# A hybrid attention and expert step: 160 prompt tokens in the first output and query pass, 96 with the samples

## The reference

```
mix = [stick_breaking attention (8 heads), sparse attention (8 heads)]       # prompt and samples
h   = layer_norm(ALPHA * x + mix @ w_out)                                     # "output pass"
q   = (h @ w_query) as 8 heads x 2 halves of 128;  s = q @ sub_keys           # "query pass"
top 16 of 128 for each half; 16 x 16 sums; top 16 of these 256                # "selection", 8 heads
    -> 128 experts per token, gate = softmax of their scores
act = gelu(u_tab[expert] . h);   y = sum over experts of gate * act * v_tab[expert]
out = layer_norm(ALPHA * h + y)
```

## Time and profile before

| | |
|---|---|
| median of 3 runs | 2565.51 us |
| the profiled execution | 2565.83 us |
| its span, first to last instruction | 2564.0 us |
| PE, DVE, POOL, ACT busy | 74%, 49%, 28%, 13% |
| moved by DMA | 964.23 MB, 376 GB/s over the span |
| u and v gathers | 288 + 288, 59.7% of the DMA time |
| chain that ended last | DMA 47%, PE 34%, DVE 8% |

### The profile page before, as it was taken

The page is one execution under the profiler, slowest core; times in us unless marked ns, Lnnn a source line. Parts: engine busy times, 40 slices in busy tenths (PEclk is TensorE's granted clock), DMA queues, the critical chain, the costliest instruction groups (busy, mean ns, idle before and its releaser), DMA issues.

```text
span 2564.0 us, 29141 instructions
## 1 busy us (share of the span) xinstructions
PE 1894.7 (74%) x9494; PEld 1079.4 (42%) x9494; DVE 1248.9 (49%) x2349; ACT 335.7 (13%) x787; POOL 719.3 (28%) x594
## 2 busy tenths in 40 slices
PE   8999999979999877757776663665563545988336
PEld 5777766544478654534554310221120002655000
DVE  0510122253048867677887535434433345477860
ACT  0000111422031000201100101101110010011011
POOL 0000000000002533334333324324534246434562
PEclk9999999989999989978999876777685665555556
DMA  9889979896349999999999999999999999999998
GB/s 397 301 344 358 371 274 379 340 374 257 121 184 361 395 409 409 408 411 412 409 409 410 410 397 410 410 397 392 416 385 397 421 421 422 421 421 414 417 420 342
DMA packets 213687, 964.23 MB, mean 376 GB/s; under 512 B 23937, under 2 KB 89474, under 8 KB 122818
## 3 DMA queue, kind: packets, MB, share of 16 engines
q0 software_dynamic: 84512, 627.05, 59.7%
q1 hardware_dynamic: 93074, 300.33, 30.7%
q10 hardware_dynamic: 35952, 35.01, 4.0%
HBM read 955.81 MB, written 14.88 MB: 379 GB/s over the span
## 4 chain that ended last, share of the span: by engine, by line
DMA 47%; PE 34%; DVE 8%; issue 4%; SPq 2%; ACTq 2%; POOL 1%; ACT 1%; POOLq 0%; DVEq 0%
DMA sb<-in_peer_u,sb 20%; DMA sb<-in_peer_v,sb 19%; PE bank L1038 14%; PE bank L1344 4%; DMA sb<-in_nsa_t 4%; DVE sb L2319 4%; PE bank L1386 4%; DMA sb<-in_nsa_v 3%; PE bank L1677 2%; PE bank L1102 2%; PE bank L1142 2%; POOL sb L2427 1%; ACTq L892 1%; DMA sb<-in_a_v 1%; SPq L613 1%
## 5 line engine op out<-in xcount | busy, mean ns | idle before, releaser
L1677 PE MATMUL bank<-sb 128*32 128x512 f32 x2304 | 475.8, 846 | 528.6 <-DMA sb<-in_peer_v,sb 509.7
L2319 DVE CUSTOM_DVE_ANT_1 sb<-sb 128x2048 f32<-128x2048 f32 x224 | 513.4, 2293 | 517.6 <-DMA sb<-in_peer_u,sb 515.3
L2427 POOL DMA_INDIRECT sb<-in_peer_v,sb x288 | 407.1, 1413 | 444.3 <-PE bank L1677 346.8
L2427 POOL DMA_INDIRECT sb<-in_peer_u,sb x288 | 304.1, 1056 | 763.5 <-DVE sb L2319 531.2
L1677 PEld LDWEIGHTS bank<-sb 128*32 128x32 f32 x2304 | 62.3, 124 | 750.1 <-DMA sb<-in_peer_v,sb 711.3
L1038 PE MATMUL bank<-sb 128*128 128x288 f32 x1408 | 351.6, 409 | 11.8 <-DMA sb<-in_w_in 11.8
L1038 PEld LDWEIGHTS bank<-sb 128*128 128x128 f32 x1408 | 266.8, 191 | 95.5 <-issue 12.2
L1429 PE MATMUL bank<-sb 128*128 128x256 f32 x1024 | 292.1, 440 | 0.8 <-ACT sb L837 0.5
L1429 PEld LDWEIGHTS bank<-sb 128*128 128x128 f32 x1024 | 250.5, 309 | 76.6 <-issue 57.9
L2319 DVE CUSTOM_DVE_ANT_0 sb<-sb 128x2048 f32<-128x2048 f32 x64 | 146.4, 2292 | 78.4 <-DMA sb<-in_peer_u,sb 74.5
L1004 ACT ACTIVATE sb<-sb 128x32 f32<-128x32 f32 x288 | 83.1, 313 | 508.0 <-PE bank L1677 301.2
(11 more groups left out here) (363 smaller groups left out, 1491.1 us busy)
## 6 DMA issues: line engine op xcount, KB each, us to landing
sb<-in_a_k SPq DMA_DIRECT2D x128, 512.0 KB, 6.9
sb<-in_a_v SPq DMA_DIRECT2D x128, 512.0 KB, 6.8
sb<-in_w_in SPq DMA_DIRECT2D x44, 1024.0 KB, 9.4
sb<-in_w_out SPq DMA_DIRECT2D x32, 1024.0 KB, 8.9
sb<-in_w_query SPq DMA_DIRECT2D x32, 1024.0 KB, 9.1
sb<-in_nsa_t SPq DMA_DIRECT2D x200, 128.0 KB, 10.0
sb<-in_nsa_t ACTq DMA_DIRECT2D x184, 128.0 KB, 14.1
sb<-in_nsa_v SPq DMA_DIRECT2D x64, 128.0 KB, 15.9
```

The costliest lines, as they stand in the source:

```text
L1677: mm = pe.matmul(bank[g % 2][32 * c:32 * c + 32, :], diag[j % 4], rows[:, 512 * c:512 * c + 512], start=(s in FIRST), stop=(s in LAST), sk ...
L2319: dve.tensor_tensor_reduce(out=u, in0=u, in1=replica(g), scale=1.0, scalar=0.0, op0=ALU.mult, op1=ALU.add, accum_out=act16[:, r % 2, j:j + ...
L2427: pool.indirect_dma_start(rows[j % 4], None, dram[table], bass.IndirectOffsetOnAxis(ap=idx, axis=0)).then_inc(full[j % 4], 16)
```

## The change

The token tiles are cut anew. Before, 256 prompt tokens were in the first output and query pass and the 32 sample rows in the second. Now the first pass has 160 prompt tokens (a tile of 128 and one of 32: groups 0 to 4) and the second has 96 prompt tokens and the 32 samples as one tile of 128 (groups 5 to 8). Groups 5 and 6 share slots 160 to 223 as groups 0 and 1 share the first 64. What follows from it:

- In `out_rows` the tile of 32 tokens is multiplied in four column strips, one k block in each; DVE adds the four parts (`prompt_rows`).
- In `query_rows` 160 columns move instead of 256; in the first three blocks, which work tile by tile, the second piece has 32 columns instead of 128.
- The second output pass has 128 rows in four strips, one token group in each; no fold of parts follows. The second query pass has 128 columns instead of 32. The norm rows that it needs are loaded for 128 partitions.
- The samples' compression, pick and attention are pulled forward and made denser: a block every 2.5 slots instead of 3, pages, window rows and weights two blocks per slot instead of one. `OUT_AT` goes from 198 to 132, `QUERY_AT` from 230 to 146; both passes take 8 slots.
- LAG is 19 instead of 22, and ACT makes each diagonal one slot ahead of its matmul.
- The last tile's prompt rows get a final norm of their own near slot 280.

The diff, cut to its core:

```diff
-LAG = 22
+LAG = 19
-TAPS_AT = (20, 72)
+TAPS_AT = 10
-PICK_AT = 82
-NSA_AT = (123, 157)
+PICK_AT = 66
+NSA_AT = (92, 111)
-        order += [("ks", h, i, NSA_AT[h] + i) for i in range(8)] + [("kw", h, i, NSA_AT[h] + 9 + i) for i in range(2)]
+        order += [("ks", h, i, NSA_AT[h] + i // 2) for i in range(8)] + [("kw", h, i, NSA_AT[h] + 4) for i in range(2)]
...
-OUT_AT = 198
-QUERY_AT = 230
+OUT_AT = 132
+QUERY_AT = 146
...
-                        sp.dma_start(smp_norm[0:NSMP, n, :], dram["norms"][n:n + 1, :].to_broadcast([NSMP, DM])).then_inc(smp_norm_in, 16)
+                        sp.dma_start(smp_norm[0:ROWS_2, n, :], dram["norms"][n:n + 1, :].to_broadcast([ROWS_2, DM])).then_inc(smp_norm_in, 16)
...
-                if t >= LAG:
-                    diagonal_of(t - LAG)
+                if LAG - 1 <= t < SLOTS_ALL + LAG - 1:
+                    diagonal_of(t - LAG + 1)
...
             def out_rows(k, tt):
+                parts, rows = (1, P) if tt == 0 else (PARTS_1, ROWS_1)
                 for kt in range(4):
-                    mm = pe.matmul(bank[3 * (n % 2) + tt][:, :], mix(4 * kq + kt)[:, P * tt:P * tt + P], w[:, kt, :],
-                                   start=(kq == 0 and kt == 0), stop=(kq == 3 and kt == 3))
+                    own = slice(rows * (kt % parts), rows * (kt % parts) + rows)
+                    mm = pe.matmul(bank[3 * (n % 2) + tt][own, :], mix(4 * kq + kt)[:, P * tt:P * tt + rows], w[:, kt, :],
+                                   start=(kq == 0 and kt < parts), stop=(kq == 3 and kt >= 4 - parts))
...
             for m in range(3, 16):
                 pe.wait_ge(q_in, max(4, m + 1))
-                query_rows(m, 0, NPROMPT).then_inc(item_used, 1)
+                query_rows(m, 0, TOK_1).then_inc(item_used, 1)
...
                 for kt in range(4):
-                    mm = pe.matmul(bank[2 + n][32 * kt:32 * kt + 32, :], smp_mix_t[:, 4 * kq + kt, :], w[:, kt, :],
-                                   start=(kq == 0), stop=(kq == 3))
+                    at = 4 * kq + kt
+                    first, last = kq == 0 and kt == 0, kq == 3 and kt == 3
+                    for own in range(0, ROWS_2, 32):
+                        rows = mix_2[:, at, own:own + 32] if own < ROWS_P else smp_mix_t[:, at, :]
+                        mm = pe.matmul(bank[2 + n][own:own + 32, :], rows, w[:, kt, :], start=first, stop=last, skip_group_check=True)
...
-                    mm = pe.matmul(bank[2 + m % 2][:, 0:NSMP], w[:, P * kt:P * kt + P], h_t[:, kt, NPROMPT:T], start=(kt == 0), stop=(kt == KT - 1))
+                    mm = pe.matmul(bank[2 + m % 2][:, 0:ROWS_2], w[:, P * kt:P * kt + P], h_t2[:, kt, :], start=(kt == 0), stop=(kt == KT - 1))
...
             def prompt_rows(n, tt):
+                parts, rows = (1, P) if tt == 0 else (PARTS_1, ROWS_1)
...
-            FIRST_GROUPS = {0: (0, 1), 1: (), 2: (0,)}
+            FIRST_GROUPS = {0: (0, 1), 1: (), 2: (GROUPS_1, GROUPS_1 + 1)}
```

More of the change, by code:

```diff
@@ L33, with place @@
 NGRP = T // NSMP
+GROUPS_1 = 5
+ROWS_1 = NSMP * (GROUPS_1 - 4)
+TOK_1 = P + ROWS_1
+ROWS_2 = T - TOK_1
+ROWS_P = NPROMPT - TOK_1
+PARTS_1 = P // ROWS_1
+def place(g):
+    if g < 4:
+        return 0, slice(32 * g, 32 * g + 32)
+    tile, row = (1, 32 * (g - 4)) if g < GROUPS_1 else (2, 32 * (g - GROUPS_1))
+    return tile, slice(row, row + 32)
 SCALE = 1.0 / float(np.sqrt(HD))
@@ L1655, in background @@
-                d = t - QUERY_AT
-                if 0 <= d < 32:
-                    query_of(d // 2, d % 2)
-                if d >= 5 and d % 2 == 1 and d < 37:
-                    score_of((d - 5) // 2)
+                if 0 <= d < 8:
+                    out_of(2 * d)
+                    out_of(2 * d + 1)
+                elif d in (12, 13):
+                    for c in range(2 * d - 24, 2 * d - 22):
+                        turn_second(c)
+                d = t - QUERY_AT
+                if 0 <= d < 8:
+                    query_of(2 * d)
+                    query_of(2 * d + 1)
@@ L2349, in collect @@
                 dve.wait_ge(v_used, LAST_OF[g] + 1)
[L2350 to L2351 removed]
+                tt, own = place(g)
                 for c in range(4):
```

518 lines of the change are left out of this document (269 added, 249 removed).

## The result

The changed kernel takes 2550.09 us (median of 5 runs, 2548.59 to 2551.97), the kernel before, in the same rounds, 2564.96 us: ratio 0.9946, 95% interval 0.9931 to 0.996. That is 14.9 us faster. Run again later, beside other kernels, it took 2549.47 us (ratio 0.9955, 0.9942 to 0.9969). The forecast was 30.9 us: right in sign, twice too large, with the time inside the stated range of 2521 to 2557.

A forecast was written before the change was run, and what follows sets the result against it. It took the kernel as bound by PE until the first gather at 753 us, then mostly by DMA bytes; -34.6 - 7 + 3.7 + 0 + 3 + 4 = -30.9 from 2565.8 gave 2535 us, range 2521 to 2557.

The forecast's parts named there:

- Output pass, -34.6: First output pass: four side-by-side strips at 0.12 us a record let the transposes begin 34.6 us sooner.
- rival 4: Output pass: the four strips run one after the other and it gains nothing, 2570 us; chance 0.01.
- Query pass, -7: First query pass: 33.7 us of PE go, but DMA bytes limit the gain to 7 us (0 to 13).
- the 0.97 named as a sign: First query pass: DMA share of 0.97 or more beside 160-column blocks of 4.3 us would show the forecast right.
- microseconds taken from PE before 753 count in full: Before the first u gather at 753 us DMA stands idle, so each us saved on PE shortens the kernel.
- Norm rows, +3.7: Second pass: sample norm rows loaded for 128 partitions add 1.57 MB at 421 GB/s, 3.7 us.
- Second passes on PE, 0: Second output and query passes: 8.7 and 8.6 us of PE per slot hide under 10.0 of DMA, 0 us.
- Rival 1: Both dense second passes run at half PE clock, +74 us, 2609 us; chance 0.08.
- Second pass on DVE, +3: Slots 154 to 182: DVE needs 5.26 us a slot against 4.98 for DMA, costing 3 us (0 to 8).
- denser stages, +4: Sample stages in slots 10 to 130: bursts of page loads with four buffers cost 4 us (0 to 15).
- Rival 2: Sample stages: the bursts starve DMA in 20 slots, 33 us lost, no change at 2564 us; chance 0.11.
- Lag, no price: Lag of 19 slots: DVE finishes weights a slot before PE uses them, so the shorter lag costs nothing.

The follow-up runs named there:

- e5: Changed kernel with the second tile's strips of output blocks 8 to 11 also moved behind the first tile: 2545.45 us.
- e1: Changed kernel with eleven useless 512-column matmuls on PE in the gap between the output pass and the transposes: 2550.99 us.
- e4: Changed kernel with the 32-token tile of the output pass multiplied one strip after another, not in four side by side: 2585.86 us.
- e2: Changed kernel with the compression of the sampled tokens' pages starting at slot 20 instead of 10, still ending at slot 87: 2554.75 us.
- e12: Changed kernel with the activation's exponential ahead of the sampled tokens' work in each ACT slot: 2549.84 us.
- e11: Changed kernel with the heads of the second selection 5 slots apart instead of 4, its pairs 10 instead of 8: 2547.36 us.
- e8: Changed kernel with the block ranking spread over twice the slots, in slots 82 to 90: 2545.85 us.
- e7: Changed kernel with LAG back at 22 instead of 19 and the last tile's final norm 2 to 5 slots later: 2547.58 us.

## Why the prediction was right in sign and twice too large

**Output pass, -34.6: mechanism right, size 5.4 short.** The first dot product stands 29.2 us sooner behind the start of the pass. The strips do run side by side (rival 4 falls), but a record takes (73.09 - 128 x 0.430) / 128 = 0.141 us in the mean, not 0.12, and tile 0 ended at 69.5 us, not 66.6: 3 us. The mean hides two prices. The 32 records in a row at the end take (73.09 - 69.54) / 32 = 0.111, and the 96 that alternate with tile 0, eight and eight, (69.54 - 55.04) / 96 = 0.151; e5's trace gives 0.109 and 0.152. The 0.12 came from a row of 16 such records in a run, not from the alternation. The norm chain was as forecast (681.30 to 690.12, 8.8 us), and so was PE's gap (5.36 for some 5). What I did not price is the clock, at 0.50 in the transposes and 1.00 again only some 14 us later: 3.1 us by e1, and e4, without a gap, has the same 32 us from there to the first dot product. The length of the gap is not the whole cause, for in e5 the clock fell behind 1.93 us as it had behind 5.36; what does it stays open. The three additions of tile 1 were hidden. That all of it counts, e4 and e5 show. One sign came true by luck: the first u gather was to stand near 719 us and stood at 719.72, but only since the span ahead of the pass was 5 us shorter by chance. From the start of the pass it is 108.1 us, for 102.0 forecast.

**Query pass, -7: this step failed.** It said that with PE done early "the sample pages and the v rows (19 slots behind u, not 22) fill the gaps", 99.5 us for what took 107. The pass was indeed shorter, though by some 20 us from the first block to the last and not 33.7: a 160-column block took 4.54 us (forecast 4.32), and the three second pieces, which were to gain nothing, lost 7.7 us, since the clock was at 0.50 to 0.65 on their 32 columns. But none of it came back: the idle time of slots 0 to 20 is 9.4 us for 8.4 before (by the packets 9.4 and, in the repeat, 7.9, for 8.3), and the share beside the blocks 0.95, not the 0.97 named as a sign. The forecast named the condition itself ("none if DVE ... stays the pace") and then took the middle of the range; its upper bound even took 3 us for sure. DVE did stay the pace: POOL waited for it before the first v gather, and in e2, whose items start as before the change, slots 0 to 20 take as long as they had. The change also put two things behind the pass that DVE had not needed so early, the gates' exponentials and the sampled item 1 (slot 16, first needed in slot 28 before); by e2 and e12 that cost little here, and it mattered only where the pass was lengthened.

**The rule "microseconds taken from PE before 753 count in full": incomplete.** I left out that 0.8 to 1.9 MB had passed under the longer output pass and now come behind it, 2 to 4.6 us. With the 7 us of the query pass this makes 9 to 12 us of a miss of 16 (medians) to 19 (profiles).

**Norm rows, +3.7:** 1.63 MB more by the page, 4.0 us at 408 GB/s; not tested alone.

**Second passes on PE, 0: right.** Rival 1 falls: the clock was up and the rate full (the output pass lies in the first window, the query pass in 1734 to 1808).

```profile
1600.00:1700.00 100.00, 77.29 (x659) 22.27 (x659) 28.89 (x35) 3.21 (x11) 30.32 (x24) 0.91 1.01 421
1700.00:1800.00 100.00, 77.32 (x611) 59.75 (x604) 52.31 (x104) 22.32 (x53) 33.79 (x26) 0.86 1.01 421
```

**Second pass on DVE, +3, and denser stages, +4: right in sum, partly for another reason.** Slots 160 to 192 are idle 6.3 us for 4.1, and e11 takes 3 of them away. In the stages behind slot 20 the idle time grew by 7 us (slots 20 to 160: 4.1 before, 11.3 after). But the main dip is not a burst of pages, which I had priced. It is DVE: ranking, head parts, group sums and the pages' own sums fall into slots 80 to 88, 5.0 us idle, and e8 gets them back. The bursts proper (slots 92 to 160) cost 5.3. That DVE is what idles the queues in slots 80 to 88 is shown by e8; for slots 160 to 192, by e11. Rival 2 (33 us) falls.

**Lag, no price: not quite.** A lag of 22 gains 2 to 6 us alone, near the noise, and none beside the other edits. I read this as the forecast's slot of margin being used up where DVE is late; it is not shown apart from e7's idle times.

The sum by the two profiles: -29.2 + 4.6 - 0 + 4.0 + 8 to 11 is -10 to -13, for -12.3 in the two profiles and -14.9 in the medians.
